# A home for the feed-forward rows at an aligned address, and one-pass constant products in seven norms

## What is computed

```python
def rmsnorm(x, g):
    xf = x.astype(jnp.float32)
    y = xf * lax.rsqrt(jnp.mean(xf * xf, axis=-1, keepdims=True) + EPS)
    return (y * g.astype(jnp.float32)).astype(x.dtype)

def swiglu(h, wg, wu, wd):
    return (jax.nn.silu(h @ wg) * (h @ wu)) @ wd

# first block, layer 0 and layer 1
x = x + hybrid_mixer(rmsnorm(x, norm_mix[l]), ...)
x = x + swiglu(rmsnorm(x, norm_ffn[0]), ...)        # layer 0, 2816 wide
x = x + moe_swiglu(rmsnorm(x, norm_ffn[1]), ...)    # layer 1, 8 experts, top 2, 3584 wide
# second block, in each layer
h = modulate(rmsnorm_2(x, norm_g[layer, 0]), sh1, sc1)
x = x + 0.5 * g1 * swiglu_2(h, ...)
h = modulate(rmsnorm_2(x, norm_g[layer, 1]), sh2, sc2)
x = x + g2 * (three_attentions(h) @ w_out[layer])
h = modulate(rmsnorm_2(x, norm_g[layer, 2]), sh3, sc3)
x = x + 0.5 * g3 * swiglu_2(h, ...)
```

## Time and profile before

| | |
|---|---|
| median of 3 runs | 2462.81 us |
| lowest, highest | 2461.85, 2464.23 us |
| profiled execution: span from first to last instruction (its only time) | 2461.3 us |
| TensorE busy | 2426.1 us, 17074 matmul records |
| VectorE busy | 2038.9 us |
| ScalarE busy | 1535.8 us |
| moved by DMA | 696.2 MB, 283 GB/s in the mean |

### The profile page before, as it was taken

One profiled execution on the slowest core, in us unless ns is written; L12 is line 12 of the kernel. 1 busy time (PEld: TensorE's weight loads), 2 busy tenths in 40 slices (PEclk: granted clock), 3 DMA queues, 4 the chain that ended last, 5 costly groups with the idle time before them and its releaser, 6 DMA issues.

```text
span 2461.3 us, 44012 instructions
## 1 busy us (share of the span) xinstructions
PE 2426.1 (99%) x17074; PEld 2210.0 (90%) x17074; DVE 2038.9 (83%) x2626; ACT 1535.8 (62%) x2090; POOL 174.7 (7%) x244
## 2 busy tenths in 40 slices
PE   9999999999999999999999999999999999999999
PEld 9999998899999998888898899988899899988998
DVE  5688866888988899999998799786898898787665
ACT  5644565777777777878776644557544544567543
POOL 2111021000000000000010111011011011010000
PEclk9999999999999999999999999999999999999999
DMA  7698554999999999999999688443687587432541
GB/s 295 229 366 309 201 185 157 398 365 384 370 382 369 383 378 394 394 390 392 385 391 372 239 319 308 158 148 127 245 319 295 220 316 293 152 129 82 218 181 76
DMA packets 136637, 696.20 MB, mean 283 GB/s; under 512 B 16528, under 2 KB 16656, under 8 KB 87728
## 3 DMA queue, kind: packets, MB, share of 16 engines
q1 hardware_dynamic: 109872, 598.79, 64.5%
q0 software_dynamic: 23424, 88.16, 9.3%
q10 hardware_dynamic: 3136, 6.43, 0.7%
HBM read 683.29 MB, written 13.24 MB: 283 GB/s over the span
## 4 chain that ended last, share of the span: by engine, by line
PE 83%; DVE 7%; ACT 4%; DMA 4%; issue 2%; POOL 0%; SPq 0%; ACTq 0%; DVEq 0%; POOLq 0%
PE ps L2460 16%; PE ps L2056 15%; PE ps L2057 14%; PE ps L2058 14%; PE ps L2627 9%; PE ps L2462 8%; DMA ring<-wstream 4%; DVE w_parts L1745 2%; DVE w_parts L1358 1%; PE ps L2592 1%; PE ps L2085 1%; PE ps L2081 1%; ACT w_parts L1147 1%; DVE a_parts L1752 1%; ACT w_parts L824 1%
## 5 line engine op out<-in xcount | busy, mean ns | idle before, releaser
L2460 PE MATMUL ps<-a_parts,w_parts 128*128 128x512 f32 x1760 | 618.9, 393 | 1.5 <-DVE a_parts L1323 1.3
L2056 PE MATMUL ps<-w_parts 128*112 128x256 f32 x1792 | 520.9, 291 | 8.9 <-DVE w_parts L1745 7.8
L1745 DVE TENSOR_TENSOR w_parts<-ring,w_parts 128x2048 fp32r<-128x2048 f32 x222 | 506.4, 2281 | 0.0
L2058 PE MATMUL ps<-w_parts 128*112 128x256 f32 x1792 | 499.0, 278 | 0.0
L2057 PE MATMUL ps<-w_parts 128*112 128x256 f32 x1792 | 499.0, 278 | 0.0
L2462 PE MATMUL ps<-a_parts,w_parts 128*128 128x256 f32 x1760 | 492.7, 280 | 0.0
L1147 ACT ACTIVATE w_parts<-ring 128x2048 fp32r<-128x2048 f32 x222 | 424.3, 1911 | 18.5 <-DMA ring<-wstream 18.3
L2460 PEld LDWEIGHTS ps<-a_parts,w_parts 128*128 128x128 f32 x1760 | 329.8, 187 | 75.5 <-issue 3.7
L2056 PEld LDWEIGHTS ps<-w_parts 128*112 128x112 f32 x1792 | 313.4, 175 | 45.3 <-issue 38.8
L2462 PEld LDWEIGHTS ps<-a_parts,w_parts 128*128 128x128 f32 x1760 | 332.3, 189 | 0.0
L2057 PEld LDWEIGHTS ps<-w_parts 128*112 128x112 f32 x1792 | 312.9, 175 | 6.5
(11 more groups left out here) (288 smaller groups left out, 4390.1 us busy)
## 6 DMA issues: line engine op xcount, KB each, us to landing
ring<-wstream SPq DMA_DIRECT2D x378, 1024.0 KB, 7.8
ring<-wstream SPq DMA_DIRECT2D x378, 512.0 KB, 5.9
proj<-astream POOLq DMA_DIRECT2D x144, 512.0 KB, 5.6
slot_rows<-branch POOLq DMA_DIRECT2D x7, 448.0 KB, 7.2
slot_out<-slot_rows POOLq DMA_DIRECT2D x1, 3136.0 KB, 14.8
sq<-slot_rows ACTq DMA_DIRECT2D x49, 64.0 KB, 5.2
slot_out<-pT ACTq DMA_DIRECT2D x49, 64.0 KB, 4.8
vtok<-crow POOLq DMA_DIRECT2D x3, 512.0 KB, 3.8
```

What stands on the lines that cost most here:

```text
L1745: nc.vector.tensor_tensor(up_lo[:, n % 2, :], ring[:, s, 0:UP], up_hi[:, n % 2, :], ALU.subtract).then_inc(up_used, 1)
L2056: mm(o, stationary[0], moving[0], start=start, stop=False, skip_group_check=True)
L2058: return mm(o, stationary[1], moving[0], start=False, stop=stop, skip_group_check=True)
L2460: mm(ps[:, bank, :], hi, a_parts[:, :, k, :], start=k == 0, stop=k == KB - 1, skip_group_check=True)
```

## The change

hid_hi and hid_lo are reserved right behind proj instead of behind top8. In norms 2, 5, 6, 7, 8, 9 and 10 the six fp32 products of ones and the cosine table are replaced by products of hid_lo (stationary) and hid_hi (moving), fp32r and so in one pass, three for each entry of a table; an entry gives the number of moving columns, the first moving column, the number of stationary columns and the first stationary column. The result goes to bank 7 as before and nobody reads it. Norms 0 and 1 keep their six products.

```diff
+KEEP_BUSY = {
+    2: [(T, 0, P, s) for s in (0, 4, 8, 16, 32, 64, 128)],
+    5: [(T, o, P, 0) for o in (4, 8, 16, 32, 64, 128, 256)],
+    6: [(T, 4, P, 4), (T, 8, P, 8), (T, 16, P, 16), (T, 2, P, 0), (T, 64, P, 64), (T, 12, P, 4), (T, 24, P, 0)],
+    7: [(T, 0, 112, s) for s in (0, 4, 8, 16, 32, 64, 128)],
+    8: [(T, 0, 64, 0), (T, 0, 32, 0), (T, 0, 96, 0), (P, 0, P, 0), (P, 16, P, 0), (T, 48, 112, 0), (T, 0, 96, 16)],
+    9: [(2 * T, 0, P, s) for s in (0, 4, 16, 64)],
+    10: [(c, 0, P, 0) for c in (192, 288, 320, 384, 448)],
+}
...
         proj = sb("proj", [P, 21, T])
+        hid_hi = sb("hid_hi", [P, 2, T], fp32r)
+        hid_lo = sb("hid_lo", [P, 2, T], fp32r)
         branch = sb("branch", [P, 3 * 4 * (16 + T)])
...
         sg, hid = sm[:, 0:2, :], sm[:, 2:4, :]
-        hid_hi = sb("hid_hi", [P, 2, T], fp32r)
-        hid_lo = sb("hid_lo", [P, 2, T], fp32r)
...
                 ins.then_inc(ss_ready, 1)
-                if n in HEADS:
+                if n in KEEP_BUSY:
+                    moving, still = (h.rearrange("p b t -> p (b t)") for h in (hid_hi, hid_lo))
+                    for cols, at, width, w_at in KEEP_BUSY[n]:
+                        for _ in range(3):
+                            mm(ps[0:width, 7, 0:cols], still[:, w_at:w_at + width], moving[:, at:at + cols],
+                               start=True, stop=True)
+                elif n in HEADS:
                     for _ in range(6):
                         mm(ps[:, 7, 0:T], ones[:, :], xT[:, 0, :] if n == 0 else C("cos"), start=True, stop=True)
```

## The result

The changed kernel takes 2471.76 us (median of four runs, 2469.35 to 2472.83), the kernel before 2462.33 (four runs, 2461.45 to 2464.23): a ratio of 1.0038, 95% interval 1.0026 to 1.0051. It is slower by 9.4 us; the forecast was 2462.0, no change.

What follows compares the result with a forecast made beforehand. TensorE, busy 2426.1 of 2461.3 us and carrying 83% of the chain, was taken as the bound. 2461.3 - 0.3 + 0 - 0.5 = 2460.5, plus 1.5 around the span, gave 2462.0 us; range 2456 to 2466.5.

Steps and rivals of the forecast that it cites:

- Part 1: Constant products in seven norms: the new ones fit under the chain over ScalarE and VectorE, cost 0.
- rival 1: Address conflict in the norms' table: 0.215 us per 256-column product, together 11.4 us, kernel 2473; chance 0.04.
- the sum of equal steps: Constant products of a norm priced as count times one spacing, such as 21 x 0.120 = 2.52 us.
- the 2.69 and 2.85 that were to show it: Sign in the norms: first product 2.69 us (norm 2) or 2.85 us after the first constant one, as now.
- The small term: First product after a norm's wait: 0.08 us extra passage might move under the cover; -0.3 us, bounds -0.6 and +0.2.
- Rival 2, the clock: TensorE idling before the first product drops the clock in seven norms: +9 to +13 us, 2471 to 2475; chance 0.02.
- Part 2 (a): Writers of hid_hi and hid_lo: the low part takes 426 ns unaligned, 0.42 us aligned; no change.
- (b): The feed-forward's 2640 down products: alignment smooths the steps, mean stays 0.120 us; 0, bounds -17.6 and +3 us.
- Rival 3: Alignment speeds the feed-forward's down products to 0.113 us or half way: -17.6 or -9 us, 2444 to 2453; chance 0.07.
- Part 2 (c): Experts' down products with the rows stationary: 0 to 5 ns gained each; -0.5 us taken, bounds -2.5 and 0.

Runs made afterwards that it cites:

- e3: The changed kernel with 32 bytes of padding ahead of hid_hi and 32 behind hid_lo: 2462.93 us, ratio 1.0001 to the kernel before.
- e12: Kernel before, small cut by 64 bytes, feed-forward rows 64 bytes lower, everything the experts use left in place: 2456.46 us, ratio 0.9979.
- e2: The changed kernel with hid_hi and hid_lo back behind top8, so only the constant products are new: 2461.46 us, ratio 0.9997 to the kernel before.
- e1: The kernel before with only the home of hid_hi and hid_lo moved, norms keeping six fp32 products: 2471.99 us, ratio 1.0036.
- e8: Kernel before with the home moved and, from chunk 2, one extra overwritten product of 32 x (c mod 8) columns ahead of the up products: 2480.11 us, one run.
- e4: The kernel before with 32 bytes of padding ahead of hid_hi and 32 behind hid_lo, in their old place: 2474.72 us, ratio 1.0049.
- e6: The kernel before with only the home moved, 16 bytes of padding ahead and padding behind to 2048 in all: 2463.68 us, one run.
- e9: The kernel before with 64 bytes of padding behind hid_lo, the rows themselves staying where they were: 2466.35 us, one run.

## Why the prediction was wrong

- **Part 1 was right in its cost of nothing.** All seven sets of constant products stay under the chain over ScalarE and VectorE, norm 9 included. Their starts are 113 to 123 ns apart for 256 columns and 225 to 236 for 512 (but the first of each set), at every address relation in the table; rival 1, the conflict at 215 ns, is out. Two details were off without harm. The first of a set is followed after 0.31 us (256 columns) or 0.42 (512), which the sum of equal steps left out; and since the set begins 0.19 us earlier, the first product comes 2.88 and 3.04 us after the first constant one instead of the 2.69 and 2.85 that were to show it. The small term was mis-sized: the product behind the first still comes 0.19 us after it in norm 2, so that stays with the wait, and the -0.3 us are not there.
- **Rival 2, the clock**, is out: the mean granted clock of the execution is 1.000, and all slices stand at 9. Its price rested on a count: the granted clock in the earlier trace rows is 1.00 in both stretches, and the 1.2 GHz of the first was inferred from 16 records where later 29 fit.
- **Part 2 (a) and (b) were right in their cost**: the low part of the rows takes 425 ns to write (426 before), and the 2640 down products keep their mean of 0.120 us. The steps did not become even, as was forecast: within a down run they vary from 117 to 125 ns, in a pattern of five, where before they varied from 115 to 125. Rival 3 is out for this home; e3 and e12 show that a mean of 0.118 can be had, at another one.
- **The step that failed** is the one by which I chose what to cost: "Those with the feed-forward rows (hid_hi, hid_lo) as the moving side", and nothing else. I priced the products that read the moved rows, and the 3520 records of the up products had no term in the sum at all; they were taken for unchanged, because their operands stay. Their pace hangs on what runs ahead of them, and 100 up runs at 0.094 to 0.1 us more are nearly 10 us, 9.2 in the sum over all up records, where the first chunks of a stage gained 0.4. No rival had it; the slower end was placed in the norms and the clock, so that its size (2471 to 2475) fitted is luck.
- **It could have been seen.** The up products of the earlier trace rows were read at one place only. The second chunk of the same stage goes at 0.353 us a pair, 1.06 for three, though in another order, and chunk 2 of the third feed-forward does so in the same order. Two paces for one form say that the pace is no property of the form; with that seen, "the rhythm changes by up to 0.006 us a pair, 1760 pairs, 11 us" would have been a rival with a price.
- **Part 2 (c)**: the second expert went from 120.35 to 119.91 us in the profiles of the two kernels, a gain of the forecast's size, but others hardly moved (119.88 to 119.91 for the fourth), and e2, with the rows in their old home, has 120.04 for the second. The experts as a whole scatter by 3 us between executions (from the first down product to the last 947.4 us in the changed kernel, 950.6 in e1 with the same addresses, 950.0 before). So this term is not measured.

The Trainium skill, "TensorE: Matmul & The Clock Gate", section "Step-by-step: what each phase is for", has two independent ports for weights and moving rows, so that a load takes no bandwidth from the running matmul; section "Back-to-back issue gap" of the same page has an isolated gap of N/2.4 + 2.5 ns. An estimate by them is 216 + 109 = 325 ns a pair, wherever things lie. That section calls the formula one for a single product and not for a stream of loads and products, and the prediction used it for a stream. The traces have 347 and 353, and 2.83, 2.85 and 2.88 us for 24 down products by the rows' address alone; the measurement decides. The runs don't show why; they show only that addresses and history matter.

## What to carry to other kernels

When a tensor is moved, the products that read it are not the only ones to cost. As this kernel shows, a dense stream of weight loads and matmuls can sit in one of several steady rhythms, and products of which no operand moved can be thrown from the fast into the slow one. Before pricing such a change, compare the spacing of one form at several places of a stage; if it has two values, the difference times the count is a rival. "Aligned like the others" at a multiple of 1024 was the worst home tried for the feed-forward itself, and the gain came from offsets found on the chip, with everything else held in place to the byte.

## What was not expected of the hardware

- One form of up pair, same operands and clock, has steady spacings of 0.347 and 0.353 us. In e8 the width of a single product ahead of it (32 or 96 columns against 160 or 224, in odd chunks from 8 on) chose between them, and the choice held for the 5 us of the run.
- 24 down products take 2.88 us with rows 96 bytes past a multiple of 128 (before) and at a multiple of 1024 (changed, e1), 2.85 at an odd multiple of 128 (e4), and 2.83 at 16 or 32 bytes past a multiple of 1024 (e6, e3) and at 32 past one of 128 (e12).
- 64 bytes of padding behind the rows, feed-forward untouched, cost three experts together 2.6 us of 360.3 (e9, one run), all of it in their up products, whose operands had not moved. Which of the tensors behind does that is left open, as is the mechanism.
- One-pass products get hardly cheaper below 256 columns: in norm 8 of the changed kernel those of 128 columns start 109 to 113 ns apart (one 60), those of 256 columns 113 to 123 in norms 2 and 5 to 8; above that the columns count, 205 ns with 448 in norm 10.
